# Rotary halves exchanged by a VectorE shuffle, and two decay terms of the forgetting attention in one eight-row matmul

## What is computed

```python
def partial_rope(t, cos, sin):              # rotates the first `rot` features of a head
    half = cos.shape[-1]
    rot = 2 * half
    t1, t2, rest = t[..., :half], t[..., half:rot], t[..., rot:]
    return concatenate([t1 * cos - t2 * sin, t1 * sin + t2 * cos, rest])

def hybrid_layer(x, ...):
    p = split_columns(rms_norm(x, norm_g) @ w_in)
    # fox: logits = q.k / sqrt(128) + F[t] - F[s],  F = cumsum(log_sigmoid(f + fb)), causal softmax, times v
    # diff: two 64-wide query/key sets per head, 16 of the 64 features rotated,
    #       (softmax(q1 k1) - lam * softmax(q2 k2)) v, then rms_norm
    # moba: 128-wide heads, 32 of the 128 features rotated; with 256 tokens there is one block of
    #       keys, so it is causal softmax attention
    # gla:  gated linear attention with a decay for each feature, then rms_norm
    mixed = concatenate([fox, diff, moba, gla]) * silu(gates)
    return x + mixed @ w_out
```

## Time and profile before

| | us |
|---|---|
| runs | 3722.03 (median), 3705.48, 3725.27 |
| profiled execution | 3721.06 |
| its span, first to last instruction | 3719.3 |
| PE busy | 3543.8 (95%) |
| DVE busy | 2565.0 (69%) |
| ACT busy | 1525.8 (41%) |
| POOL busy | 985.5 (26%) |
| mean granted TensorE clock | 0.972 of full speed |

### The profile page before, as it was taken

One profiled execution on the slowest core, in us unless ns is written; L12 is line 12 of the kernel. 1 busy time (PEld: TensorE's weight loads), 2 busy tenths in 40 slices (PEclk: granted clock), 3 DMA queues, 4 the chain that ended last, 5 costly groups with the idle time before them and its releaser, 6 DMA issues. The chain is left out here.

```text
span 3719.3 us, 57141 instructions
## 1 busy us (share of the span) xinstructions
PE 3543.8 (95%) x21802; PEld 3106.5 (84%) x21802; DVE 2565.0 (69%) x3362; ACT 1525.8 (41%) x1581; POOL 985.5 (26%) x793
## 2 busy tenths in 40 slices
PE   8988989999999999888899999999999999999998
PEld 7977878888888889877788888888878888888887
DVE  7577577767676765776777676767766766676665
ACT  4432344333333544334443333435443443444442
POOL 2082423202021420643223030214321004140004
PEclk9988999999999999989999999999999999999999
DMA  6432445555555544324455555555443444443444
GB/s 221 136 116 89 159 158 181 175 197 174 198 174 186 193 167 157 120 91 137 157 182 183 189 184 188 184 178 191 170 159 125 147 166 170 161 154 126 147 162 143
DMA packets 93808, 604.20 MB, mean 162 GB/s; under 512 B 10416, under 2 KB 13648, under 8 KB 33104
## 3 DMA queue, kind: packets, MB, share of 16 engines
q1 hardware_dynamic: 92736, 598.78, 46.9%
q10 hardware_dynamic: 912, 3.25, 0.2%
HBM read 599.88 MB, written 2.10 MB: 162 GB/s over the span
## 5 line engine op out<-in xcount | busy, mean ns | idle before, releaser
L521 PE MATMUL bank<-H,whi 128*128 128x512 f32 x6304 | 2258.7, 402 | 46.0 <-DVE H L1456 20.5
L525 PE MATMUL bank<-H,wlo 128*128 128x256 f32 x7552 | 2138.5, 283 | 0.0
L982 ACT ACTIVATE whi<-raw 128x2048 fp32r<-128x2048 f32 (+4 forms) x636 | 1098.7, 1728 | 1201.8 <-DMA raw<-in_slabs_down 281.1
L1376 DVE TENSOR_TENSOR wlo<-raw,whi 128x2048 fp32r<-128x2048 f32 (+4 forms) x636 | 1330.8, 2093 | 248.3 <-ACT whi L982 245.1
L521 PEld LDWEIGHTS bank<-H,whi 128*128 128x128 f32 x6304 | 1191.4, 189 | 354.7 <-issue 37.3
L525 PEld LDWEIGHTS bank<-H,wlo 128*128 128x128 f32 x7552 | 1446.5, 192 | 0.6
L521 PE MATMUL bank<-G,whi 128*128 128x512 f32 x1408 | 497.8, 399 | 0.0
L439 POOL TENSOR_TENSOR sqtmp<-tmp 128x256 f32<-128x256 f32 x88 | 216.6, 2461 | 928.7 <-DVE tmp L1897 928.7
L523 PE MATMUL bank<-H,whi 128*128 128x256 f32 (+1 forms) x1248 | 375.5, 301 | 34.4 <-DVE H L1445 20.8
L525 PE MATMUL bank<-G,wlo 128*128 128x256 f32 x1408 | 395.5, 281 | 0.0
L524 PE MATMUL bank<-H,whi 128*128 128x256 f32 (+1 forms) x1248 | 363.2, 291 | 0.0
(11 more groups left out here) (306 smaller groups left out, 2466.5 us busy)
## 6 DMA issues: line engine op xcount, KB each, us to landing
raw<-in_slabs_up SPq DMA_DIRECT2D x176, 1024.0 KB, 4.9
raw<-in_slabs_down SPq DMA_DIRECT2D x128, 704.0 KB, 4.0
raw<-in_slabs_wo SPq DMA_DIRECT2D x32, 1024.0 KB, 4.9
raw<-in_slabs_pg SPq DMA_DIRECT2D x32, 1024.0 KB, 4.9
raw<-in_slabs_gates SPq DMA_DIRECT2D x32, 1024.0 KB, 4.9
raw<-in_slabs_wout SPq DMA_DIRECT2D x32, 1024.0 KB, 4.9
raw<-in_slabs_ret SPq DMA_DIRECT2D x24, 1024.0 KB, 5.0
raw<-in_slabs_sc SPq DMA_DIRECT2D x24, 1024.0 KB, 4.9
```

Of the source, the lines that this page charges most:

```text
L521: pe.matmul(b[0:r.m, :], whi[:, n % RAW, w], r.src[:, k, :], start=k == 0, stop=False)
L525: last = pe.matmul(b[0:r.m, 0:T], wlo[:, n % RAW, w], r.src[:, k, 0:T], start=False, stop=k == r.kt - 1)
L982: act.activation(whi[:, n % RAW, 0:w], raw[:, n % RAW, 0:w], ACT.Copy).then_inc(S("hi_ready"), 1)
L1376: dve.tensor_tensor(wlo[:, n % RAW, 0:w], raw[:, n % RAW, 0:w], whi[:, n % RAW, 0:w].bitcast(F32), ALU.subtract).then_inc(S("lo_ready"), 1)
```

## The change

In block 2 the halves of a rotary pair are exchanged by VectorE's `stream_shuffle`, a permutation that is the same in each group of 32 partitions, straight from `z` into the lower half of `tmp`. The sign moves into the sine table. `rotate_pair`, its waits and its two matrices go, and `pX` is no longer part of this. VectorE's `rope_pair` now has three operations in place of two, and waits for GpSimd's cosine part only ahead of the last. Waits of TensorE on `o_normed` that stood at the rotations move to the next user of `pX`, and those on `rope_pair` at users of `pX` that touch no rotated chunk go.

For fox the decay input is written twice, to eight partitions (two a head). For each head `fox_keys` holds, in the head's two rows, a constant and F, by two columns of a constant table, and zero in the others. The queries' side `fox_cum` has F and a constant in each pair. One matmul with eight rows then adds both terms. `fox_sums` has a memset, a scan and five scalings. The constants are 246 columns narrower.

```diff
-            sin[base + i] = np.sin(ang[:, i % (rot // 2)].astype(np.float64))
+            sin[base + i] = np.sin(ang[:, i % (rot // 2)].astype(np.float64)) * (-1.0 if i < rot // 2 else 1.0)
...
-    blocks["rot_diff"] = rotation(8, 64)
-    blocks["rot_moba"] = rotation(16, 128)
...
+    fox = np.zeros((P, 2 + 2 * HEADS))
+    for h in range(HEADS):
+        cum, one = 32 + 2 * h, 33 + 2 * h
+        fox[cum, 0] = float(P) ** 0.5
+        fox[one, 1] = 1.0
+        fox[one, 2 + 2 * h] = -float(P) ** 0.5
+        fox[cum, 3 + 2 * h] = 1.0
+    blocks["fox_rows"] = fox
...
-            pick = C("ident")[32:32 + HEADS, 32 + h:33 + h].to_broadcast([HEADS, T])
             for a, b, q0, w in ((0, P, 0, P), (P, 3 * P, P, T)):
                 pe.matmul(pS[:, a:b], q[:, q0:q0 + P], kk[:, 0:w], start=True, stop=False)
-                pe.matmul(pS[:, a:b], fox_cum[:, q0:q0 + P], pick[:, 0:w], start=False, stop=False)
-                last = pe.matmul(pS[:, a:b], pick[:, q0:q0 + P], fox_cum[:, T:T + w], start=False, stop=True)
+                last = pe.matmul(pS[:, a:b], fox_cum[:, q0:q0 + P], fox_keys[:, h, 0:w], start=False, stop=True)
...
-        def rotate_pair(lhs, key, chunk):
-
-            pe.wait_ge(S("evac"), by[key].first + chunk - CHUNK[key[0]] + 2)
-            if nth("rope_pair") > 1:
-                pe.wait_ge(S("rope_pair"), cnt["rope_pair"] - 1)
-            for o in range(2):
-                last = pe.matmul(pX[:, o * T:(o + 1) * T], lhs, z[:, chunk + o, :], start=True, stop=True,
-                                 skip_group_check=True)
-            last.then_inc(S("rotated"), 1)
...
-            if s == 27:
-                pe.wait_ge(S("o_normed"), 4 * l + 2)
-            if 27 <= s < 31:
-                rotate_pair(C("rot_diff"), ("diff", l), DIFF_ROPES[s - 27])
...
             if s in (31, 33):
-                pe.wait_ge(S("rope_pair"), 8 * l + 4)
+                pe.wait_ge(S("o_normed"), 4 * l + 2)
...
-            if s in (38, 39, 40, 44):
-                if s == 38:
-                    pe.wait_ge(S("values"), 8 * l + 6)
-                if s == 44:
-                    pe.wait_ge(S("o_normed"), 4 * l + 4)
-                rotate_pair(C("rot_moba"), ("moba", l), MOBA_ROPES[min(s, 41) - 38])
             if s == 41:
-                pe.wait_ge(S("rope_pair"), 8 * l + 7)
+                pe.wait_ge(S("values"), 8 * l + 6)
                 o_sums()
...
             if s in (45, 46):
-                pe.wait_ge(S("rope_pair"), 8 * l + 8)
+                pe.wait_ge(S("o_normed"), 4 * l + 4)
...
-            link(dve.tensor_scalar(fox_cum[:, 0:T], fox_cum[:, 0:T], float(P) ** 0.5, None, ALU.mult))
-            link(dve.tensor_scalar(fox_cum[:, T:2 * T], fox_cum[:, 0:T], -1.0, None, ALU.mult), "fox_cum")
+            rows = C("fox_rows")[fox_at, :]
+            for h in range(HEADS):
+                dve.tensor_scalar(fox_keys[:, h, :], fox_cum[:, 0:T], rows[:, 2 + 2 * h:3 + 2 * h],
+                                  rows[:, 3 + 2 * h:4 + 2 * h], ALU.mult, ALU.add).then_inc(S("fox_keys"), 1)
+            dve.wait_ge(S("fox_keys"), HEADS * (l + 1))
+            link(dve.tensor_scalar(fox_cum[:, 0:T], fox_cum[:, 0:T], rows[:, 0:1], rows[:, 1:2], ALU.mult, ALU.add),
+                 "fox_cum")
...
-        def rope_pair(chunk, sin):
-
-            dve.wait_ge(S("rotated"), nth("rot"))
-            dve.wait_ge(S("rope_cos"), nth("rope_cos"))
-            if cnt["rope_cos"] == 1:
+        def rope_pair(key, chunk, swap, sin):
+
+            dve.wait_ge(S("evac"), by[key].first + chunk - CHUNK[key[0]] + 2)
+            if nth("rope_cos") == 1:
                 dve.wait_ge(S("tables_in"), 32)
-            turned = tmp[:, 0:2, :]
+            pair, turned = z[:, chunk:chunk + 2, :], tmp[:, 0:2, :]
             both = sin.rearrange("p (a t) -> p a t", a=1).to_broadcast([P, 2, T])
-            link(dve.tensor_tensor(turned, pX[:, :].rearrange("p (a t) -> p a t", a=2), both, ALU.mult))
-            link(dve.tensor_tensor(z[:, chunk:chunk + 2, :], decays, turned, ALU.add), "rope_pair")
+            link(dve.stream_shuffle(turned, pair, swap))
+            link(dve.tensor_tensor(turned, turned, both, ALU.mult))
+            dve.wait_ge(S("rope_cos"), cnt["rope_cos"])
+            link(dve.tensor_tensor(pair, decays, turned, ALU.add), "rope_pair")
```

More of the change, by code:

```diff
@@ L142, in packed_vectors @@
         elif name == "fox_fb_2":
-            packed[32:32 + HEADS, at] = v
+            packed[32:32 + 2 * HEADS, at] = np.repeat(v, 2)
         else:
@@ L203, in misc_columns @@
     both[:, 0:16] = w[:, B_GA:B_GA + 16]
-    both[:, 32:32 + HEADS] = w[:, B_FF:B_FF + HEADS]
+    both[:, 32:32 + 2 * HEADS] = np.repeat(w[:, B_FF:B_FF + HEADS], 2, axis=1)
     return both
@@ L350, in _build @@
     decays = tmp[:, 2:4, :]
-    fox_f, fox_ln, fox_cum = sqacc[32:32 + HEADS, :], sqtmp[32:32 + HEADS, :], rstd[32:32 + HEADS, :]
+    fox_at = slice(32, 32 + 2 * HEADS)
+    fox_f, fox_ln, fox_cum = sqacc[fox_at, :], sqtmp[fox_at, :], rstd[fox_at, :]
+    fox_keys = z[fox_at, 0:HEADS, :]
+    SWAP_8 = list(range(8, 16)) + list(range(8)) + list(range(16, 32))
+    SWAP_16 = list(range(16, 32)) + list(range(16))
     def advance(beside, stages=2):
@@ L1623, in decay_inputs @@
                                   ALU.add).then_inc(S("decay_x"), 1)
-            dve.tensor_scalar(fox_f, small[32:32 + HEADS, :], col("fox_fb_2", l)[32:32 + HEADS], None,
+            dve.tensor_scalar(fox_f, small[fox_at, :], col("fox_fb_2", l)[fox_at], None,
                               ALU.add).then_inc(S("fox_x"), 1)
@@ L1751, in after_split @@
             if 27 <= s < 31:
-                rope_pair(DIFF_ROPES[s - 27], C("sin_diff"))
+                rope_pair(("diff", l), DIFF_ROPES[s - 27], SWAP_8, C("sin_diff"))
             if s in (31, 33, 35, 37):
@@ L1755, in after_split @@
             if s in (38, 39, 40, 44):
-                rope_pair(MOBA_ROPES[min(s, 41) - 38], C("sin_moba"))
+                rope_pair(("moba", l), MOBA_ROPES[min(s, 41) - 38], SWAP_16, C("sin_moba"))
             if s in (42, 43):
```

## The result

The changed kernel takes 3683.78 us (median of 6 runs, 3681.26 to 3687.04), the kernel before 3712.02 beside it (6 runs, 3705.48 to 3725.27). The ratio is 0.9908, 95% interval 0.9889 to 0.9927: faster by 0.9%. The profiled execution of the changed kernel has a span of 3681.0 us, that of before 3719.3, so the two traces differ by 38.3 us, and half of that is not where the change is.

What follows compares the result with a forecast made beforehand. The prediction took TensorE (PE), busy 95%, to bound the kernel. Rotations 13.6 plus fox 7.1 less waits of 0.6 and 0.8 gave 19.3 us, so 3721.06 became 3701.8 us, a 0.52% gain; range 3688 to 3712.

Steps and rivals of the forecast that it cites:

- Part 4: Remaining effects: extra fox_sums scalings hidden by a VectorE wait, GpSimd unchanged, narrower constants saving only hidden transfer time: 0.
- Part 1: Block 2, between slabs: 16 rotations leave TensorE at 0.85 us each, 13.6 us, all on the path.
- Part 2: Fox heads of block 2: two matmuls fewer a head, 6.6 us, plus 0.5 at low clock: 7.1 us.
- rival that eight rows save nothing: Fox heads: the eight-row matmul costs what two four-row ones did, giving 3708.9 us; chance 0.06.
- Part 3: Rotary pairs on VectorE: one added shuffle per pair, mostly covered, giving back 0.6 and 0.8 us.
- S: Time of one 128x512 shuffle on VectorE including loading the permutation: taken as 0.8 us, range 0.35 to 1.5.
- narrow places: Where the shuffle outruns VectorE's cover: diff head 0 (0.6 us in both layers) and the pair at s = 44 (0.8).
- first diff head: After slab 31, VectorE is late with diff head 0's probabilities; TensorE waits 0.3 us more a layer, 0.6 in all.
- scores of moba head 0 after slab 45: Cover of 0.83 us shrinks by 1.65, so TensorE waits 0.8 us in the first layer, none in the second.
- fox_sums: Iteration 22: five scalings for two, each at most 0.35 us, about 1.1 us more, hidden by a 3.00 us wait.
- rival of the clock: Low-clock stretches after the one-column sums in both layers vanish, saving 4.9 us more: 3696.9 us; chance 0.19.

Runs made afterwards that it cites:

- e5: The kernel before with only an unused 32-byte tile ahead of z, so that z, y and G start 32 bytes later: 3700.84 us, ratio 0.9935.
- e17: The kernel before with only the rotations changed to shuffles, and gaps putting H and G 32 bytes past the weight tiles: 3667.95 us, ratio 0.9879.
- e18: The kernel before with only fox changed to eight-row matmuls, and gaps putting H and G 32 bytes past the weight tiles: 3675.49 us, ratio 0.9892.
- e15: The kernel before with gaps alone, putting H and G 32 bytes past the weight tiles within 128: 3682.75 us, ratio 0.9907.
- e16: The changed kernel with gaps putting H and G 32 bytes past the weight tiles within 128: 3664.35 us, ratio 0.9850 to the kernel before.
- e4: The changed kernel with 246 unused columns behind its constants, so all tiles lie as in the kernel before: 3707.23 us, ratio 0.9959 to the kernel before.
- e7: The changed kernel once more, no edit, on another chip: 3683.67 us, ratio 0.9896 to the kernel before.
- e1: The kernel before once more, no edit: 3723.57 us, ratio 1.0001 to the kernel before.

## Why the prediction was wrong, point by point

3701.8 us was forecast and 3683.78 came, below the range that began at 3688. The sum for block 2 came out right (19.3 forecast, 18.4 measured at an even pace), in part because errors in it cancel, as the points below show. The step that failed is the last clause of Part 4: "The narrower constants save a small part of one transfer at the start, which hides behind the first slabs: 0." It priced the constants as data that is loaded. Their width also sets where every tile behind them starts, and e5 measured this at 23.9 us, more than the whole of the change. No rival named it. The rows of before had the length of a pair in them (rows 5: L521 at 2876.66, L525 at 2876.90, and the next group 0.12 us on, so 0.36), and `w_o` of its first layer ran at 346.7 in the same trace. So both lengths were there to be read, but not what sets them.

**Part 1, the rotations: right.** 13.6 us less 1.4 given back; e17 measured 13.3 by the medians and 12.6 from the mark. Between slabs 28 and 29, where a rotation stood, TensorE now has:

```profile
2845.84 0.28 PE L535 MATMUL bank<-H,wlo 128*128 128x256 f32 x1
2845.96 0.49 PE L626 MATMUL pT<-cst,soft 128*128 128x128 f32 x3
2846.21 0.48 PE L531 MATMUL bank<-H,whi 128*128 128x512 f32 x1
```

What comes next starts 0.12 us after the slab's last matmul, as forecast; it is a group of transposes, and the slab follows it with nothing between.

**Part 2, fox: a term was too large.** The eight-row matmuls take 2838.35 - 2837.94 = 0.41 and 2839.60 - 2838.98 = 0.62 us, the four-row ones 0.31 to 0.33 and 0.51 to 0.54 (rows 4 and above). So four more rows cost 0.1 us each time. That is the upper bound of the forecast, which took 0 as "the end the few rows are nearest to". The trace can't tell what the 0.1 is made of: besides the rows, the second operand is now `z` instead of a column read with a stride of zero. The head saves 0.66 instead of 0.83, eight heads 5.3 instead of 6.6 us. The 0.5 us for head 0 at the lower clock came in the first layer, where it now runs at the upper level (2810.32 on), and was lost in the second, where it now runs at the lower. The rival that eight rows save nothing is out: e18 won 5.8 by the medians.

**Part 3, the shuffle: right in size.** S is 0.728 us and 0.01 for loading the permutation, 0.74 against the 0.8 taken. The estimate from the Trainium skill (VectorE: DVE Perf Modes, The perf-mode tier table: one element a cycle, about 2400 ns for 2048) was 0.6 to 0.8; by its rule of one element a cycle the trace agrees.

**The narrow places.** VectorE at the end of iteration 27 and the start of 28:

```profile
2844.88 0.69 DVE L1695 TENSOR_TENSOR tmp<-tmp,cst 128x512 f32<-128x512 f32 x1
2845.60 0.69 DVE L1697 TENSOR_TENSOR z<-tmp 128x512 f32<-128x512 f32 x1
2846.33 0.69 DVE L1381 TENSOR_REDUCE z<-bank 128x256 f32<-128x512 f32 x1
```

Slab 28 was done at 2845.96 (the transposes above begin) and VectorE took its bank at 2846.33, without idle time: late by 0.4 us, where 0.1 was forecast, and the 1.54 us of rows 8 are used up. At the first diff head:

```profile
2873.70 0.55 PE L626 MATMUL pT<-cst,soft 128*128 128x128 f32 x3 [1.76 <-DVE soft L1491]
```

TensorE waits 1.76 us in the first layer, where 0.3 was forecast. The total of the waits at the diff heads rose by 5.7 - 2.9 = 2.8 us against 0.6. The place and the mechanism were right, the size was too small. It isn't a matter of one execution: at an even pace the same total is 3.6 in e15, 4.9 in e17 (rotations alone) and 6.3 in e16 (both), so the rotations add 1.3 and the fox part, in the first layer alone, 1.4 more. The forecast took 0.85 us a pair off VectorE's cover and did not count that the fox head behind slab 27 gets shorter as well, by 0.66. That this makes the 1.4 fits the 0.4 above but isn't shown, since the second layer has the same edit and no such wait. The other place, the scores of moba head 0 after slab 45:

```profile
2961.95 0.60 PE L743 MATMUL pX<-cst,z 128*128 128x128 f32 x4
2962.39 0.82 PE L618 MATMUL pS<-z 128*128 128x128 f32 x4
```

No wait, where 0.8 us was forecast: the pair that it needs was ended at 2961.96 (L1697, start 2961.27 and 0.69 us), 0.43 ahead of need. What the forecast overlooked is a wait of VectorE for ScalarE in that iteration of before, ahead of the split, which is gone in the changed kernel and pays for the shuffle (before, then after):

```profile
2985.65 2.29 DVE L1376 TENSOR_TENSOR wlo<-raw,whi 128x2048 fp32r<-128x2048 f32 x1 [1.04 <-ACT whi L982]
```

```profile
2957.57 2.28 DVE L1364 TENSOR_TENSOR wlo<-raw,whi 128x2048 fp32r<-128x2048 f32 x1
```

The two errors make 2.8 - 1.4 = 1.4 us together.

**fox_sums.** The scalings of eight rows take 0.399 us where at most 0.35 was given; no wait for `fox_cum` shows, so they are hidden as said.

**The clock.** In the profiled changed kernel the stretches after the one-column sums are still there:

```profile
2811.00:2814.70 3.70, 3.70 (x14) 3.13 (x14) 3.48 (x5) 2.91 (x6) 0.00 (x0) 0.54 0.12 49
3323.00:3330.00 7.00, 7.00 (x20) 5.04 (x20) 4.32 (x9) 3.68 (x6) 0.00 (x0) 0.52 0.25 107
```

Against rows 6 they have changed places, the short one in the first layer and the long one in the second, and nothing is won. So the rival of the clock, nearest of all to the result with 3696.9, is not what made the difference. It isn't dead either: in e16 one of the stretches is gone and in e18 both. Whether they come differs between the kernels, for a cause that isn't shown, and it is worth 1.8 us a time.

**The sum again.** With the terms as measured: rotations 13.6, fox 5.3, given back 2.8, clock 0 in the changed kernel and 1.8 in e16. That is 16.1 us, or 17.9 for e16. e4, at the placement of before, measured 16.1 by its median, and e16 less e15 18.4. The forecast's 19.3 was thus 3.2 too high in its own terms, and a stretch of low clock that happened to be missing in e16 made up 1.8 of it: luck, for that part. (The marks give more for before and after, 19.6, and for e4, 21.5: in block 2, too, loops over `H` at distance 0 take one pace or the other, from trace to trace.)

**The spread of before.** The runs of before, 3705.48 to 3725.27 in the first three, were taken as noise about the median. With `H` at distance 0 the pace of some loops differs between traces of one program (after and e7, before and e1), and this is a likely source. It was argued from the traces of single executions, and not shown for the untraced runs.

What stays open: why 32 bytes past the weights is the fast distance and what makes the others slower; why the up projections, with `H` at 0, follow the place of `G`; why `G` and `H` behave unlike at 96; and why other loops over `H` at 0 change pace from trace to trace. No kernel had `G` at 0 behind an up projection at 346.7, so whether `G` at 0 is slow by itself or goes on at the pace it finds is open too. Distances other than multiples of 32 were not tried, nor one of the two weight tiles moved against the other.

## What to carry to other kernels

An edit that changes the width of a tile can move all tiles declared behind it, as it did here, and in a kernel that TensorE bounds this can outweigh the edit. In a kernel like this one, compare two versions only with the tiles at the same places, or at a place where both run even, and read the distance from matmul to matmul in a loop that wasn't touched before you put a difference down to the code. To size a change, take two landmarks that both programs have and compare stretches; a difference ahead of the first landmark has another cause.

## What the runs showed of the hardware

A pair of float32r matmuls with 512 and 256 moving columns, back to back at the upper clock, takes 346.7 ns with the moving operand 32 bytes past the weights within 128 bytes, and up to 353.3 at the other multiples of 32, as the mean of a loop. Three unused tiles that put both moving operands there, with nothing else changed, took the kernel before from 3721.4 to 3682.8 us (e15); 32 unused bytes ahead of one operand took it from 3724.7 to 3700.8 (e5). Four rows more cost a float32 matmul of 128 or 256 columns 0.1 us here. A shuffle of 128x512 float32 within 32 partitions takes 0.728 us, 5% more than a product of the same shape (0.692).
